# RWKV inverse on 64x64 diagonal blocks of all eight heads in one tile, the two 128-token chunks level by level in turn

## The reference

```python
def step(state, inp):
    r_t, w_t, k_t, v_t, kk_t, a_t = inp
    sa = jnp.einsum('bhij,bhj->bhi', state, -kk_t)
    state = (state * w_t[:, :, None, :]
             + sa[..., None] * (kk_t * a_t)[:, :, None, :]
             + v_t[..., None] * k_t[:, :, None, :])
    y_t = jnp.einsum('bhij,bhj->bhi', state, r_t)
    return state, y_t
```

## Time and profile before

| | us |
|---|---|
| median of three runs (1792.18 to 1795.31) | 1793.51 |
| the profiled execution, its time | 1790.86 |
| the profiled execution, its span | 1789.1 |
| PE busy | 1610.8 (90%) |
| DVE busy | 381.4 (21%) |
| ACT busy | 297.9 (17%) |
| mean granted TensorE clock | 0.945 of full speed |

### The profile page before, as it was taken

One profiled execution on the slowest core, in us unless ns is written; L12 is line 12 of the kernel. 1 busy time (PEld: TensorE's weight loads), 2 busy tenths in 40 slices (PEclk: granted clock), 3 DMA queues, 4 the chain that ended last, 5 costly groups with the idle time before them and its releaser, 6 DMA issues.

```text
span 1789.1 us, 19200 instructions
## 1 busy us (share of the span) xinstructions
PE 1610.8 (90%) x7790; PEld 853.6 (48%) x7791; DVE 381.4 (21%) x692; ACT 297.9 (17%) x470; POOL 49.2 (3%) x89
## 2 busy tenths in 40 slices
PE   6997677876789999999999999999999999999998
PEld 3875466654633333333333333333333387598643
DVE  2335422123231211211111121212121123311002
ACT  2224201111111211211111111111111123100000
POOL 3000111010000000000000000000000000000000
PEclk9999667777779999999999999999999999999999
DMA  9515012203539999999999999999999953343330
GB/s 356 182 47 211 30 65 95 95 0 136 246 156 428 427 429 429 429 428 428 428 428 428 429 428 428 429 429 429 428 428 429 412 212 136 135 148 141 141 141 24
DMA packets 75033, 503.15 MB, mean 281 GB/s; under 512 B 5278, under 2 KB 8496, under 8 KB 50416
## 3 DMA queue, kind: packets, MB, share of 16 engines
q1 hardware_dynamic: 72240, 498.22, 67.9%
q10 hardware_dynamic: 2752, 4.34, 0.7%
HBM read 501.49 MB, written 1.05 MB: 281 GB/s over the span
## 4 chain that ended last, share of the span: by engine, by line
PE 54%; DMA 21%; DVE 2%; ACT 1%; issue 0%; ACTq 0%; SPq 0%; DVEq 0%
DMA ring<-in_w_gate_up 21%; PE psum L922 14%; PE psum L958 8%; PE psum L1168 5%; PE psum L1183 5%; PE psum L990 3%; PE psum L886 2%; PE psum L870 2%; PE psum L513 2%; PE psum L820 2%; PE psum L1125 2%; PE psum L1193 2%; PE psum L915 1%; PE psum L1140 1%; PE psum L1100 1%; PE psum L1006 0%
## 5 line engine op out<-in xcount | busy, mean ns | idle before, releaser
L922 PE MATMUL psum<-ring,work 128*64 128x512 f32 x2048 | 457.5, 597 | 44.2 <-DMA ring<-in_w_gate_up 44.2
L922 PEld LDWEIGHTS psum<-ring,work 128*64 128x64 f32 x2048 | 140.5, 137 | 359.3 <-issue 269.5
L958 PE MATMUL psum<-ring,work 128*64 128x512 f32 x1024 | 226.8, 595 | 1.6
L1871 DVE TENSOR_SCALAR work<-psum 128x512 f32<-128x512 f32 x32 | 22.1, 691 | 628.5 <-PE psum L922 628.5
L958 PEld LDWEIGHTS psum<-ring,work 128*64 128x64 f32 x1024 | 71.2, 137 | 136.7 <-issue 130.2
L1168 PE MATMUL psum<-xT,ring 128*128 128x256 f32 x448 | 96.9, 379 | 0.0
L1429 ACT ACTIVATE work<-work 128x512 f32<-128x512 f32 x32 | 20.1, 630 | 440.6 <-DVE work L1871 440.6
L1168 PEld LDWEIGHTS psum<-xT,ring 128*128 128x128 f32 x448 | 85.0, 190 | 11.5
L576 PE MATMUL psum<-hT,ring 128*128 128x256 f32 (+1 forms) x368 | 80.4, 380 | 2.8 <-ACT hT L1258 2.8
L1183 PE MATMUL psum<-ring 128*128 128x512 f32 x192 | 82.6, 592 | 0.0
L576 PEld LDWEIGHTS psum<-hT,ring 128*128 128x128 f32 (+1 forms) x368 | 68.3, 186 | 15.0 <-ACT hT L1258 3.1
(11 more groups left out here) (392 smaller groups left out, 1472.2 us busy)
## 6 DMA issues: line engine op xcount, KB each, us to landing
ring<-in_w_gate_up SPq DMA_DIRECT2D x128, 2048.0 KB, 32.0
ring<-in_w_down SPq DMA_DIRECT2D x72, 2048.0 KB, 35.3
ring<-in_w_ada SPq DMA_DIRECT2D x12, 2048.0 KB, 10.5
ring<-in_w_up SPq DMA_DIRECT2D x8, 2048.0 KB, 7.5
ring<-in_w_in SPq DMA_DIRECT2D x6, 2048.0 KB, 11.1
ring<-in_w_out SPq DMA_DIRECT2D x4, 2048.0 KB, 7.7
ring<-in_w_in_sb SPq DMA_DIRECT2D x4, 2048.0 KB, 22.6
ring<-in_w_mem_kv SPq DMA_DIRECT2D x1, 2048.0 KB, 9.1
```

The source lines that it names most:

```text
L922: ins = mm(B(1 + u)[CAP * h:CAP * (h + 1), :], xe[:, k % 4, k // 4, :], w[:, k % 2, c0:c0 + 512], start=False, stop=k == KT - 1)
L958: last = mm(B(3)[CAP * h:CAP * (h + 1), :], act[:, k % 4, k // 4, :], w[:, k % 4, 512 * h:512 * (h + 1)], start=k == 0, stop=k == KT - 1)
```

## The change

It does seven things.

1. One tile holds all eight heads: a 64x64 diagonal block of every head, with the first block of the chunk in partitions 0 to 63 and the second in 64 to 127, so that a level of a whole chunk is again a 128x512 tile. Each product of a level is 16 matmuls of 64x64x64 (eight heads, two blocks; the operands of the second block lie in partitions 64 to 127) in place of 4 matmuls of 128x128x128.
2. The levels of the two chunks alternate: PE does level l's first product for chunk 0 and then for chunk 1, then the two corrections of chunk 0, then those of chunk 1. Ten level steps take the place of twenty.
3. The off-diagonal 64x64 block (`off`) is copied out at the setup and is used in the solve in place of the last `bt`; the solve takes the first half of the tokens and then the second.
4. The scores for `ktr` move behind the first product of levels 1 to 4; each chunk has a tile of its own for `ktr`, `atr`, `x_inv`, `xt_inv`, `bt` and `y_inv`.
5. The eight late `w_ada` chunks leave the levels. Four go into the loop of the moba attention (one per pass), two into the solves of chunks 0 and 1, two into the group norm.
6. `mods` and `sc2` are finished after `y_ready`, and SP waits for `y_ready` itself.
7. `lvl` moves into the ring, compact copies of the masks are added on POOL at the start, and several semaphores are merged.

The core of the diff:

```diff
-            for gi in range(4):
-                for l in range(1, 7):
-                    n = 6 * gi + l - 1
...
+            for l in range(1, 6):
+                for c in range(TT):
                     if l == 1:
-                        g.wait_ge(S("atr_ready"), gi + 1)
-                    if n >= 2:
-                        g.wait_ge(S("bt_used"), n - 1)
-                    g_.tensor_tensor(bt[n % 2], atr[:, :, 0:P], lvl[:, l:l + 1, :].broadcast_to([P, 4, P]),
-                                     ALU.mult).then_inc(S("bt_ready"), 1)
+                        g.wait_ge(S("kk_out"), 2 * c + 1)
+                    else:
+                        g.wait_ge(S(f"bt_used{c}"), l - 1)
+                    g_.tensor_tensor(bt[c], diag[c], lvl_c[:, l:l + 1, :].broadcast_to([P, 8, HD]), ALU.mult)\
+                        .then_inc(S(f"bt_ready{c}"), 1)
...
+            wkv_setup(0, 0, 2, 4)
+            wkv_setup(1, 6, 2, 0)
+            lv = [(4, 5, 6), (0, 1, 7)]
+            for l in range(1, 6):
+                for c in range(TT):
+                    pe.wait_ge(S(f"x_ready{c}"), l)
+                    pe.wait_ge(S(f"bt_ready{c}"), l)
+                    for q in range(8):
+                        for a0 in (0, HD):
+                            last = mm(B(lv[c][0])[a0:a0 + HD, q * HD:(q + 1) * HD], bt[c][a0:a0 + HD, q, :],
+                                      x_inv[c][a0:a0 + HD, q, :], start=True, stop=True)
+                    last.then_inc(S(f"bt_used{c}"), 1)
+                if l < 5:
+                    pe.wait_ge(S("atr_ready"), 2)
+                    if l > 1:
+                        pe.wait_ge(S("ktr_ready"), l - 1)
+                    wkv_keys((l - 1) // 2, (l - 1) % 2)
+                for c in range(TT):
+                    pe.wait_ge(S(f"y_copied{c}"), l)
+                    pe.wait_ge(S(f"xt_ready{c}"), l)
+                    for q in range(8):
+                        for a0 in (0, HD):
+                            last = mm(B(lv[c][1])[a0:a0 + HD, q * HD:(q + 1) * HD], y_inv[c][a0:a0 + HD, q, :],
+                                      xt_inv[c][a0:a0 + HD, q, :], start=True, stop=True)
+                    last.then_inc(S(f"xtp{c}"), 1)
...
+            for l in range(1, 6):
+                for c in range(TT):
+                    ve.wait_ge(S(f"xtp{c}"), l)
                     if l < 5:
+                        ve.wait_ge(S(f"xp{c}"), l)
+                        V.tensor_tensor(x_inv[c], x_inv[c], q8(B(lv[c][2])), ALU.subtract).then_inc(S(f"x_ready{c}"), 1)
+                    V.tensor_tensor(xt_inv[c], xt_inv[c], q8(B(lv[c][1])), ALU.subtract).then_inc(S(f"xt_ready{c}"), 1)
```

More of the change, by code:

```diff
@@ L678, in moba_scores, with ada_product, ada_turn @@
                 last.then_inc(S("moba_s"), 1)
+            def ada_product(x, bank):
+                n = 8 + x
+                arrived(n)
+                for k in range(KT):
+                    q = 32 * (k % 4)
+                    last = mm(B(bank)[q:q + 32, :], silc[:, k, :], slot8(pro_slot(n))[:, k, :],
+                              start=k < 4, stop=k >= 4)
+                    if k % 4 == 3:
+                        last.then_inc(S("halves_used"), 1)
+            def ada_turn(x, bank):
+                pe.wait_ge(S("ada_copied"), x + 1)
+                for j in range(4):
+                    last = tr(B(bank)[:, j * P:(j + 1) * P], ada_late[x % 2][:, j * P:(j + 1) * P])
+                last.then_inc(S("ada_turned"), 1)
             moba_scores(0)
+            pe.wait_ge(S("mem_kv"), 2)
             for i in range(RT):
@@ new lines, in wkv_keys @@
+            def wkv_keys(c, half):
+                for q, par_, m, p0 in heads:
+                    if m // 2 == half:
+                        last = mm(B(2 + par_)[:, (m % 2) * T:(m % 2 + 1) * T], ki[p0:p0 + HD, m, c, :],
+                                  kr[p0:p0 + HD, m, c, :, :].rearrange("p a b -> p (a b)"), start=True, stop=True)
+                last.then_inc(S("k_scores"), 1)
+            pe.wait_ge(S("moba_oc"), RT)
+            pe.wait_ge(S("moba_tc"), RT)
+            pe.wait_ge(S("ada_summed"), 8)
@@ L762, in _ @@
+            for c in range(TT):
+                if c == 0:
+                    pe.wait_ge(S("ktr_ready"), 4)
+                else:
+                    pe.wait_ge(S("s0_ready"), 1)
+                for q, par_, m, p0 in heads:
+                    h = 2 * m + par_
+                    o = B(2 + par_)[:, m * HD:(m + 1) * HD]
+                    last = mm(o, ktr[c][:, q, 0:P], vtok[:, c, h * HD:(h + 1) * HD], start=True, stop=c == 0)
                     if c:
@@ L788, in _ @@
-                last.then_inc(S("yo_done"), 1)
+                if c == 0:
+                    for c_ in range(TT):
+                        pe.wait_ge(S(f"xt_ready{c_}"), 6)
+                ada_product(8 + c, 7)
+                if c:
+                    pe.wait_ge(S("yo_copied"), 1)
+                pe.wait_ge(S("rr_a"), c + 1)
+                pe.wait_ge(S("rr_d"), c + 1)
+                for q in range(8):
+                    for a0 in (0, HD):
+                        last = mm(B(0)[a0:a0 + HD, q * HD:(q + 1) * HD], xt_inv[c][a0:a0 + HD, q, :],
+                                  rr[a0:a0 + HD, q, :], start=True, stop=True)
@@ new lines, in _ @@
+                last.then_inc(S("w_done"), 1)
+                wkv_out(c)
+                ada_turn(8 + c, 7)
+                pe.wait_ge(S("w_copied"), 2 * c + 1)
+                for q in range(8):
+                    last = mm(B(1)[HD:P, q * HD:(q + 1) * HD], off[c][0:HD, q, :], uu[0:HD, q, :],
+                              start=True, stop=True)
+                last.then_inc(S("w_done"), 1)
+                pe.wait_ge(S("w_copied"), 2 * c + 2)
+                for q in range(8):
+                    last = mm(B(5)[HD:P, q * HD:(q + 1) * HD], xt_inv[c][HD:P, q, :], w2[HD:P, q, :],
+                              start=True, stop=True)
@@ L1377, in _, with q8 @@
-            gsq = view(tok_f, 0, [RT, T])
-            gmean = view(tok_f, 1024, [RT, T])
+                A(yT[:, 4 + i, :], B(5)[:, 0:T], ACT.Copy).then_inc(S("moba_oc"), 1)
+            def q8(v, n=8):
+                return v.rearrange("p (q t) -> p q t", q=n)
+            for c in range(TT):
+                ac.wait_ge(S("kk_scores"), c + 1)
+                for par_ in range(2):
+                    last = A(diag[c][:, 4 * par_:4 * par_ + 4, :], q8(B([0, 6][c] + par_)[:, 0:T], 4), ACT.Copy)
+                last.then_inc(S("kk_out"), 1)
+                for par_ in range(2):
+                    last = A(off[c][0:HD, 4 * par_:4 * par_ + 4, :], q8(B([0, 6][c] + par_)[0:HD, T:2 * T], 4), ACT.Copy)
+                last.then_inc(S("kk_out"), 1)
```

366 lines of the change are left out of this document (182 added, 184 removed).

## The result

| | before | changed |
|---|---|---|
| median, us | 1792.85 (1791.72 to 1795.31, 4 runs) | 1666.83 (1665.22 to 1668.00, 4 runs) |
| ratio | | 0.9295, 95% interval 0.9279 to 0.9311 |
| profiled execution: time / span, us | 1790.86 / 1789.1 | 1665.22 / 1663.5 |
| mean granted clock | 0.945 | 0.974 |

The kernel became 7.0% faster. The first rival, both gains together, is what happened.

The account below looks back on a forecast made before the run. Weight stream bounds the expert loop, so savings before `y_ready` pass on. Setups 12.5, levels 54.8, solves 42 and `w_ada` 2.5 make 111.8 against 205.3 us, 93.5 less: 1700 us predicted, range 1668 to 1745.

Parts of the forecast that it names:

- The first rival: Two streams and full clock together: 0.9 to 1.3 us per level product, 1674 us at 0.95; chance 0.25.
- What bounds the kernel: Expert loop runs at the weight stream's pace; time saved before `y_ready` passes on one for one, 82.7 us before experts.
- The unit p: Time of one level product, 16 matmuls or 32 records of 64x64x64: taken as 1.8 us, bounds 0.85 and 3.4.
- The lower bound of 0.85: Level product time in us if both blocks run beside each other at full clock.
- Counting two ways to the middle and one to each end: Reason for 1.8 us a product: either gain alone leads there, both or neither to the bounds.
- rows 6 and 7: Earlier trace rows: operands in different partition halves run beside each other, 0.069 us a record; scatter takes half one stream's time.
- Levels: 28 products, 50.4 us, plus `ktr` scores, 4.4: 54.8 us, with PE's queue setting the pace.
- 4 lost to DVE: In the levels at 0.95 us a product, 4 us of the 30 saved go to waits for DVE.
- Setups: Two chunks one behind the other, small and 128-column matmuls: 12.5 us against 30.9 before.
- Solves: Chunk 0 17 us, chunk 1 24, hand-over 1: 42 us against 60.5 before.
- `w_ada`: Late chunks' products add 2 us to the moba loop's four passes and 0.5 to the group norm.
- The range: 1668 to 1745 us, cutting off the rivals' extremes, together 0.2.

Follow-up runs that it names:

- the second profile: The changed kernel unaltered, profiled again with the later experiments: 1662.05 us, ratio 0.9287 to the kernel before.
- the grouped kernel: Changed kernel with the 128-row matmuls of chunk 1's solve (first product and outputs) before the 64-row ones: 1655.17 us, ratio 0.9230.
- the last kernel: Changed kernel with key scores moved between the chunks' corrections and chunk 1's solve matmuls grouped by row count: 1648.43 us, ratio 0.9197.

## Why the prediction was wrong, step by step

1. **What bounds the kernel** was right. The expert stream is unchanged, the way from `y_ready` to the experts is 82.8 us (82.7), and each microsecond of the stage arrived at the end.
2. **The unit p** is the step that failed. I took p = 1.8 us, "what one of the two gains alone (two streams, or full clock) gives", and it is 0.935: both gains hold at once. The lower bound of 0.85, from the two halves of the earlier trace rows at full clock, came closest. What moved me off it, that no long row starts records faster than 84 ns, was no evidence: that window holds other forms, 128 rows with 128 or 256 columns, so it shows what they needed and no floor. Counting two ways to the middle and one to each end treated two questions as coins to toss, when rows 6 and 7 had answered one of them (but for the bank that the two blocks share, which they don't test), and the clock in full queues (1.00 in the earlier trace rows) spoke on the other. With p = 0.935 and all other terms as forecast, the sum would have given 1700 - 35 x 0.865 = 1670, inside the range.
3. **Levels**: 28 x (1.8 - 0.935) = 24.2 us less than forecast, and 4.0 given back: 2.4 in waits for DVE (four of 0.45 and one of 0.62) and 1.6 in seams between products. That gives 34.6, and 34.45 is measured. The first rival's "4 lost to DVE" has the right size by luck: only 2.4 of it is DVE's. That the queue would be PE's was right by a thin margin; the product done twice and the moved scores show it from both sides.
4. **Setups**: 5.25 less, of which 5 x 0.865 = 4.3 is p. These products run at 18 to 21 ns a record, faster than p says, and 1.44 us of PE's time is idle before the second L750.
5. **Solves**: 12.2 for chunk 0 (forecast 17) and 24.6 for chunk 1 (forecast 24, and 1 for the hand-over). Chunk 0 is under in every term, since the clock was full: first product 1.9 (3.0), `w_ada` and turn 2.4 (3.0), three steps with their waits 4.8 (6.5), outputs 3.0 (4.5). In chunk 1 the turns of 128 and 64 rows were priced rightly from the earlier trace rows, 0.36 us a pair at full clock, but the sum is close in part by luck: the first product (6.9, forecast 5.8) and `w_ada` with its turn (4.2, forecast 3.0) were longer, since the clock fell to half in them, and the steps (5.0, forecast 6.5) and outputs (8.5, forecast 9) shorter.
6. **`w_ada`**: forecast 2 us more in the moba loop and 0.5 in the group norm; both became shorter, by 3.3 and 1.35 (by 2.1 and 1.3 in the second profile). The sign was wrong for both. I had priced the product against the gap and not asked what a fuller queue does to the clock of the 32 us around it.
7. **The range.** Its low end, 1668, cut off the better half of the first rival though the bound of p, 0.85, was mine. The first rival's 1674 at p = 0.95 lay 7 us over the result. Step 6 makes 7.2 of that (3.3 + 1.35, and the 2.5 forecast); setups and solves gave 4.5 more than p accounts for, and the 5.2 us by which the moba loop began late stand against those.

The prediction weighed two rules. By the Trainium skill, TensorEngine Tiling (Array Packing), Restrictions and Gotchas, different row tiles can't use one PSUM bank at the same time, so blocks that write one bank would have gained nothing over one stream. The trace disagrees, p is 0.935 with both blocks in one bank, and 1.50 where they stand apart. By the Trainium skill, TensorE: Matmul & The Clock Gate, Back-to-back issue gap, p would have been 2.0, as an estimate, with 62 ns a record, if hardware decoding is off. No run shows whether it is. A matmul of the code is two records; even so it takes 58 ns in a level and 37 to 42 in a setup, so no such floor shows.

**Still open.** Why the granted clock falls in the solves of one execution and not in those of another: the changed kernel's five later runs spread from 1661.36 to 1669.78, the grouped kernel's six fall in two sets of three (1647.84 to 1650.94 and 1659.40 to 1663.19), and in the profiles of this kernel and of its reorderings the first solve product of chunk 1 ran at a mean of 0.50, of 0.71 to 0.80, or of 1.00. So how much of the last kernel's 13.6 us is the order itself and how much the clock that came with it is only split by one profile of each. Whether a level could use four streams, as the setup does, wasn't tried, and how the 127 us divide among the smaller matmuls, the fewer level steps and the moved `w_ada` chunks isn't known beyond the two shares above (about 14 us for the two blocks in turn, 12 to 15 for the two chunks).

## What to carry to other kernels

Small matmuls were cheap here where neighbours in the queue differed in the half of the partitions they read or write: put the loop over the halves inside. Keep matmuls of 128 rows and of 64 rows apart, in runs. Where a row answers a question, take its answer for the sum, and don't average it with rows of other forms; a slow row is only a floor when its form is the one that you will run. Fill PE's waits with work that has to be done anyway, and count that the clock may rise for all that is around it.

## What the runs showed of the hardware that I had not expected

- 64x64x64 float32 records at full clock: one stream 58 ns each, two streams 29 (levels, 930 records in 34.5 us with everything else in them), setup products with both halves varied 18 to 21 ns. At half clock two streams needed 1.76 us for 32, 55 ns each.
- 16 records of 128 rows and 16 of 64 rows in turn: 5.8 us at full clock. One kind behind the other: 2.05 to 2.96.
- Four `w_ada` products put into the waits of a loop with clock 0.69 made it 0.89 to 1.00 and the loop 1.4 to 2.7 us shorter than without them (nine profiles against one).
